# A two-layer decoder trunk on one core: TensorE's share of the next work is put behind each expert unit instead of ahead of it

## The reference

```python
for l in range(DEPTH):                      # 2 layers
    x = x + mixer_l(rmsnorm(x))             # l=0: GLA + stick-breaking attention; l=1: MoBA + RG-LRU
    x = x + memory_cross_attention(...)
    x = x + peer_ffn(rmsnorm(x), ...)

def peer_ffn(xn, wq, subkeys, u, v):        # for each token and each of 8 heads
    s1, i1 = lax.top_k(s[:, :, 0], K)       # K = 16
    s2, i2 = lax.top_k(s[:, :, 1], K)
    cand = s1[..., :, None] + s2[..., None, :]
    top_s, pos = lax.top_k(cand, K)         # 16 experts out of 16384
    g = softmax(top_s)
    act = gelu(einsum('td,thkd->thk', xi, u[eidx]))
    return einsum('thk,thkd->td', g * act, v[eidx])
```

## Time and profile before

| | us |
|---|---|
| median of 3 runs | 1734.56 |
| the profiled execution | 1735.07 |
| its span, first to last instruction | 1733.3 |
| TensorE busy | 1351.0 (78%) |
| VectorE busy | 986.3 (57%) |
| ScalarE busy | 717.1 (41%) |
| GpSimd busy | 620.3 (36%) |
| moved by DMA | 670.07 MB, mean 387 GB/s |

### The profile page before, as it was taken

How to read it: one execution, slowest core, us unless ns; L and a number is a source line. 1 busy time by engine, 2 the same in 40 slices (tenths; PEclk the granted TensorE clock), 3 DMA queues, 4 the chain that set the end, 5 groups by cost and what they waited for, 6 DMA issues and landing times.

```text
span 1733.3 us, 24052 instructions
## 1 busy us (share of the span) xinstructions
PE 1351.0 (78%) x8582; PEld 691.1 (40%) x8582; DVE 986.3 (57%) x2437; ACT 717.1 (41%) x1987; POOL 620.3 (36%) x516
## 2 busy tenths in 40 slices
PE   3998979879797859878797669888797567766766
PEld 2776955536364315345364116345363111111111
DVE  2241378674457856564556866564559955445443
ACT  1241145654542534563543344563544433333332
POOL 0000033244333334233333444333334456555652
PEclk7998989989899988989898679999899676667665
DMA  8424599999999999999999999999999999999995
GB/s 339 151 93 170 183 422 423 416 407 414 420 424 421 421 422 421 423 421 421 421 424 421 421 411 421 423 421 420 422 421 414 421 418 421 422 420 422 420 422 242
DMA packets 84825, 670.07 MB, mean 387 GB/s; under 512 B 9552, under 2 KB 9824, under 8 KB 11360
## 3 DMA queue, kind: packets, MB, share of 16 engines
q0 software_dynamic: 73728, 536.90, 74.7%
q1 hardware_dynamic: 10976, 131.61, 18.6%
HBM read 667.43 MB, written 1.05 MB: 386 GB/s over the span
## 4 chain that ended last, share of the span: by engine, by line
DMA 38%; PE 34%; DVE 13%; ACT 6%; issue 5%; POOL 3%; SPq 0%; POOLq 0%; ACTq 0%; DVEq 0%; PEldq 0%
DMA arena<-in_experts,idxT 37%; PE psum L552 33%; DVE arena L1577 6%; POOL arena L1977 3%; DMA sinT<-in_positions 2%; ACT cst L1013 1%; ACT L1013 1%; ACT gains L1013 1%; DVE red L1546 1%; DVE cst L1538 1%; ACT ring L1013 1%; ACT gelus L1013 1%; ACT L1018 1%; DVE cst L1544 0%; PE psum L932 0%
## 5 line engine op out<-in xcount | busy, mean ns | idle before, releaser
L1977 POOL DMA_INDIRECT arena<-in_experts,idxT x512 | 620.1, 1211 | 1084.1 <-PE psum L552 808.4
L552 PE MATMUL psum<-arena,cst 64*64 64x512 f32 (+1 forms) x4102 | 696.0, 763 | 325.9 <-ACT cst L1013 325.5
L1577 DVE CUSTOM_DVE_ANT_0 arena<-arena,xrow 128x1024 f32<-128x1024 f32 x512 | 621.6, 1223 | 475.1 <-DMA arena<-in_experts,idxT 473.8
L552 PEld LDWEIGHTS psum<-arena,cst 64*64 64x64 f32 (+1 forms) x4102 | 129.4, 155 | 725.0 <-ACT cst L1013 650.4
L1013 ACT ACTIVATE gelus<-red 128x1 f32<-128x1 f32 x512 | 103.5, 202 | 731.3 <-DVE red L1577 730.4
L552 PEld LDWEIGHTS psum<-hT,ring 128*128 128x128 f32 x2368 | 284.2, 197 | 98.6 <-issue 92.4
L552 PE MATMUL psum<-hT,ring 128*128 128x128 f32 x2368 | 306.2, 286 | 6.4 <-DVE hT L1421 2.5
L1013 ACT ACTIVATE cst<-cst,gains 128x128 f32<-128x128 f32 x512 | 206.3, 403 | 16.8
L1013 ACT ACTIVATE gains<-gelus,gateT 128x1 f32<-128x1 f32 x512 | 150.8, 295 | 20.3 <-DVE gateT L1555 3.5
L552 PEld LDWEIGHTS psum<-mixT,ring 128*128 128x128 f32 (+1 forms) x592 | 71.1, 195 | 26.0 <-issue 22.7
L552 PE MATMUL psum<-mixT,ring 128*128 128x128 f32 (+1 forms) x592 | 78.3, 286 | 1.9 <-issue 1.2
(11 more groups left out here) (225 smaller groups left out, 856.1 us busy)
## 6 DMA issues: line engine op xcount, KB each, us to landing
ring<-in_pq SPq DMA_DIRECT2D x16, 2048.0 KB, 11.8
ring<-in_ev_out SPq DMA_DIRECT2D x4, 2048.0 KB, 10.1
ring<-in_xq SPq DMA_DIRECT2D x4, 2048.0 KB, 11.5
ring<-in_xo SPq DMA_DIRECT2D x4, 2048.0 KB, 11.7
arena<-in_experts,idxT POOLq DMA_INDIRECT x512, 15.7
ring<-in_od_out SPq DMA_DIRECT2D x4, 2048.0 KB, 11.6
ring<-in_ev_sq SPq DMA_DIRECT2D x2, 2048.0 KB, 9.5
ring<-in_ev_sk SPq DMA_DIRECT2D x2, 2048.0 KB, 12.6
```

The source lines that it names most:

```text
L552: return nc.tensor.matmul(out, lhsT, rhs, start=start, stop=stop)
L1577: V.tensor_tensor_reduce(out=ut, in0=ut, in1=xrow[:, u // PAIRS, :], scale=1.0, scalar=0.0, op0=ALU.mult, op1=ALU.add, accum_out=dots[:, k ...
L1977: nc.gpsimd.indirect_dma_start(slot[slot_of(u)], None, d["experts"], bass.IndirectOffsetOnAxis(ap=idxT[:, u:u + 1], axis=0))\
```

## The change

In `experts` on TensorE the generators are stepped behind the products of the unit (and behind `back`), not ahead of them, for every unit. The counter gets the same values as before, so the same pieces are issued in the same order; only the place of the products of the units among them moves. Nothing is changed on the other engines, in the numbers of the beats, or in the semaphores.

```diff
                 for k in range(PAIRS):
                     u = t * PAIRS + k
-                    if u or l:
-                        clock[0] = l * UNITS + u + 1
-                        for f in fronts:
-                            next(f, None)
                     pe.wait_ge(weighed, l * UNITS + u + 1)
                     v = slot[slot_of(u)][:, D:2 * D]
...
                     if previous and k == BACK_LAG + 1:
                         back(*previous)
-                    if u == l == 0:
-                        clock[0] = 1
-                        for f in fronts:
-                            next(f, None)
+                    clock[0] = l * UNITS + u + 1
+                    for f in fronts:
+                        next(f, None)
```

## The result

The changed kernel takes 1761.32 us (median of 4 runs, 1760.29 to 1762.11), the kernel before in the same session 1734.52 us (4 runs, 1733.10 to 1735.07). The ratio is 1.0155, with a 95% interval from 1.0138 to 1.0173: 26.8 us slower. The forecast was 1744.0, 9.6 us slower, in a range up to 1751. The direction is right, the size is off by a factor of almost three.

The account below looks back on a forecast made before the run. The prediction took the DMA engines, full from about 215 us but thinly queued from 340 to 380, as the bound: 3.0 + 1.5 + 0.8 + 1.5 + 2.5 + 1.0 - 0.7 = 9.6 us slower, 1744 us, range 1735 to 1751.

Parts of the forecast that it names:

- The turn of 3.0 us: From 240 to 340 us unit (1.0) and front (2.0) alternate on TensorE; every front ends 3.0 us later.
- the four rounds: Stick-breaking rounds at 274.78, 293.32, 308.15, 325.63 us: TensorE idles 1.5, 0.8, 1.5, 2.5 us, making later fronts later still.
- with fronts 3.0 us later it waits 3.0 us more: ScalarE, reading the scores in the stick-breaking rounds, waits 3.0 us more for TensorE, and VectorE behind it.
- Start and end of the program cost nothing either way: First front with work comes at unit 3, the last ends long before the last unit: no cost.
- The clock: Upper bound: new waits bring TensorE's low clock to the nine levels, 9 x 0.9 = 8 us on top, 1752.
- the 10.3 of the forecast: Lateness when the GLA levels begin: 9.3 us after the rounds plus 1.0 for unit 33 put before front 33.
- In the levels VectorE is the slower one: I take no more there: In the nine GLA levels VectorE is slower than TensorE, so no further lateness was added.
- Everywhere else a delay of a few us is eaten by the queue: Outside the thin stretch, 340 to 380 us, queued gathers hide delays of a few us: no loss.
- from 450 us on all is the same picture 9 to 10 us later: Sign in the changed profile: the shift standing at 450 us stays the same to the end.
- My third rival: Slower still: lateness empties the queue in later tiles (6 us) or the clock falls in the levels (8), about 1751; chance 0.08.
- Given back, -0.7: Holes in the DMA rate from 395 to 405 us are filled by the lag, giving back 0.7 us.
- The Trainium skill's rule that I set beside the sum: GpSimd transfer: about 2.0 us fixed plus bytes at 436 GB/s, 4.4 us per 1 MiB; loss would be 7.3 us.

Follow-up runs that it names:

- the kernel with the later readers: The changed kernel with ScalarE's and VectorE's fronts one unit later too: 1734.32 us, ratio 1.0004 to the kernel before.
- the spare products of that run: The changed kernel with 2 spare 128x128 products behind each TensorE front from 34 to 41 (GLA levels): 1758.33 us, ratio 1.0148.
- the kernel with half the bytes and later readers: The kernel before, fetching only the u rows (4 KB), with ScalarE's and VectorE's fronts one unit later: 1447.32 us, against 1513.68 with half the bytes alone.

## Why the prediction was wrong in size

**The turn of 3.0 us and the four rounds: right for TensorE, wrong for ScalarE's waits.** The distance to the readers shrank by one turn, and TensorE's idle times in the rounds sum to 6.7 us where 6.3 were forecast; the kernel with the later readers takes the loss away. But “with fronts 3.0 us later it waits 3.0 us more” failed in the last two rounds, where ScalarE waits 1.51 and 0.81 us. The prediction moved the fronts and left the units that ScalarE does ahead of these copies in place, though TensorE's idle times make them late too.

**“Start and end of the program cost nothing either way”: wrong for the start.** It rested on the point that the fronts begin at unit 3. But behind the first front with work, the column sums, TensorE now has nothing to do until the next diagonal, and it idles 2.99 us. This alone puts unit 4 only 0.3 us late (243.34 against 243.04). Then unit 4 and the front behind it run at the low clock, 1.98 and 3.78 us where 1.09 and 2.05 are usual, 2.6 us more, and unit 5 is 2.9 us late. Unit 8 is done 3.0 us late. That it is no accident of one execution shows when each trace is counted from the start of its own unit 2 on TensorE: to the end of unit 8 the changed kernel takes 25.2 us, six others with these fronts behind take 25.2 to 25.5 and three more 23.1, 24.5 and 26.5; the kernel before takes 22.1, and so does the changed kernel with the mixer alone put back ahead.

**The clock: named as a bound and then left out.** I counted it for the levels alone, and not at all in the forecast. It cost 2.6 us at the start, 1.6 at 341.42 (3.62 against 2.05) and 1.7 in the levels. The 14.4 us by which the first level starts late on TensorE (366.07 against 351.65) are the 10.3 of the forecast, about 3.0 of the start, 1.6 of this front, 0.4 of the rounds, less 0.9 that I can't place.

**“In the levels VectorE is the slower one: I take no more there”: the step that failed.** The term was put at nothing, and VectorE lost 3.7 us there, 1.7 by the clock and 2.0 still there at full clock. VectorE is indeed the busier engine (4.79 of 5 us from 355 to 360 before), but that settles nothing. What matters is whether TensorE's level is finished while VectorE and ScalarE do the unit, or begins when they have. I had asked this question for the rounds and not for the levels, where it came up nine times and cost a wait six times.

**“Everywhere else a delay of a few us is eaten by the queue”, and so “from 450 us on all is the same picture 9 to 10 us later”: the other step that failed, and the largest.** The rates of 416 and 413 GB/s show it, and the kernel with units 1 to 47 behind puts 5.6 us there by the medians, 9.4 by the traces. My third rival had this (6 us for two tiles of layer 1, at 0.08) and the bound of the clock, but as alternatives. They came together: 9.6 forecast, with 3.0 of the start, 1.6 and 3.7 of front and levels, and 5.6 of the later tiles is 23.5 of 26.8; with 9.4 for the last it is 27.3 of the 27.4 of the profiled execution. The size of the last term isn't known better than that, so the second match is in part luck. Terms of one sign and one mechanism add; a range that takes them in one at a time is too narrow.

**Given back, -0.7:** not seen as such. In the changed trace the rate from 320 to 400 us is 325 GB/s, not about 360.

The Trainium skill's rule that I set beside the sum (page “DMA: Bandwidth & Descriptors”, “Anatomy of one DMA — SWDGE (gpsimd) path”) would have made the loss 2.3 us smaller. No gather was as quick as its estimate of 4.4 us, but in the changed kernel one landed in 5.5 us, so my “each gather is taken up almost when it comes” was off by 1.2 us for the shortest. This slack would have lowered the forecast; the loss came out larger all the same, by the other terms. The Trainium skill's clock rule (“TensorE: Matmul & The Clock Gate”, Part 1: an idle array falls back to 1.2 GHz) agrees with the fronts of 3.78 and 3.62 us behind the idle times of 2.99 and 2.49 us; behind those of 1.47, 1.29 and 1.47 us the next fronts ran at full speed (2.05, 1.92 and 1.98 us).

**What stays open.** Whether the losses of the generators add, which four runs of each don't settle. Which of the fronts from unit 48 on cost the 5.6 to 9.4 us: the keys cost 0.6 alone and the 3.8 of putting them ahead is within the noise. And how much of the 2.0 us in the levels at full clock is due to the spare products of that run.

## What to carry to other kernels

In a ring of engines, an instruction's place is priced by the distance to its reader, and a step that moves one engine's work by one unit should be followed through every kind of work that the engine hands on, not only through the one that shows waits already. Ask of each: is it finished while the other engines do their part, or does it begin only then? Where the DMA engines bind, much of such a loss is hidden behind the queued gathers, so the same edit cost 1.5% in one kernel and 5.9% in another whose gathers move half the bytes; and moving the readers by the same unit took it all back where it was tried, with all the bytes.

## What the hardware showed that I had not expected

With rows of 4 KB the DMA engines were as good as full at a lower rate. In the kernel with half the bytes and later readers, near its end (columns as in the earlier trace rows):

```profile
1380.00:1430.00 50.00, 38.01 (x284) 7.28 (x280) 42.75 (x70) 31.33 (x105) 35.76 (x33) 1.00 0.97 360
```

A share of 0.97 at 360 GB/s, where rows of 8 KB gave 421 GB/s at 1.01. And two spare 128 x 128 products a level, 0.71 us of work in some 2.6, went with a granted clock of 1.00 where it had been 0.50 to 0.71.
